# Mixing stage of a six-layer transformer forward pass: B projections, compression and value tiles ahead of the attention units, gate and branch tiles woven in between

## The reference

```
n = rms_norm(h, norm_g)
aq, ak, av, bq, bkc, bvc, bks, bvs, bkw, bvw, bgate, cq, ck, cv, ga, gb, gc = split(n @ w_in)
ya = diff_attention(aq, ak, av)                 # 4 heads, two softmaxes each
yb = nsa_attention(bq, compress(bkc), compress(bvc), bks, bvs, bkw, bvw, sigmoid(bgate))   # 8 heads, 3 kinds
yc = swa_sink_attention(cq, ck, cv)             # 8 heads
merged = sigmoid(ga)*(ya @ wb[0]) + sigmoid(gb)*(yb @ wb[1]) + sigmoid(gc)*(yc @ wb[2])
h = h + merged @ w_out
```

## Time and profile before

| what | value |
|---|---|
| median of three runs | 3616.49 us (3616.34 to 3617.01) |
| profiled execution, its own time | 3612.1 us |
| its span | 3610.3 us |
| mean granted TensorE clock | 0.959 of 2.4 GHz |
| TensorE busy | 3432.8 us, 95% |
| VectorE busy | 1848.2 us, 51% |
| ScalarE busy | 1561.2 us, 43% |
| GpSimd busy | 161.0 us, 4% |

### The profile page before, as it was taken

The page is one execution under the profiler, slowest core; times in us unless marked ns, Lnnn a source line. Parts: engine busy times, 40 slices in busy tenths (PEclk is TensorE's granted clock), DMA queues, the critical chain, the costliest instruction groups (busy, mean ns, idle before and its releaser), DMA issues.

```text
span 3610.3 us, 42172 instructions
## 1 busy us (share of the span) xinstructions
PE 3432.8 (95%) x17691; PEld 2906.6 (81%) x17691; DVE 1848.2 (51%) x2378; ACT 1561.2 (43%) x1908; POOL 161.0 (4%) x253
## 2 busy tenths in 40 slices
PE   8999999859999999999999999999999999999998
PEld 6898888647888888787988788878887788878886
DVE  4455454564454564544554545524545545434545
ACT  4344444334444444443344343356444443454444
POOL 0000000020000000000000000033000000131000
PEclk9999999879999999999999999869999999789999
DMA  6545555414555445554555455503554555413553
GB/s 205 189 165 178 187 186 189 144 35 150 189 180 189 161 162 189 177 187 163 170 174 188 151 188 169 165 24 98 174 187 164 178 193 158 130 47 117 186 189 112
DMA packets 329835, 576.39 MB, mean 160 GB/s; under 512 B 45034, under 2 KB 148561, under 8 KB 329517
## 3 DMA queue, kind: packets, MB, share of 16 engines
q1 hardware_dynamic: 327116, 566.71, 47.2%
q0 software_dynamic: 2384, 6.63, 0.6%
q10 hardware_dynamic: 144, 0.35, 0.0%
HBM read 571.53 MB, written 1.08 MB: 159 GB/s over the span
## 4 chain that ended last, share of the span: by engine, by line
PE 90%; DVE 6%; ACT 3%; issue 1%; DMA 0%; POOL 0%; DVEq 0%; SPq 0%; ACTq 0%; POOLq 0%
PE up L1584 19%; PE up L1586 19%; PE up L1585 19%; PE acc L1584 7%; PE acc L1586 7%; PE acc L1585 7%; DVE w_lo L891 2%; ACT w_hi L513 2%; PE acc L1742 1%; PE up L1847 1%; PE up L2055 1%; PE acc L1749 1%; PE acc L1743 1%; PE acc L1653 0%; PE acc L1669 0%
## 5 line engine op out<-in xcount | busy, mean ns | idle before, releaser
L891 DVE TENSOR_TENSOR w_lo<-raw,w_hi 128x2048 fp32r<-128x2048 f32 x543 | 1244.2, 2292 | 1334.9 <-ACT w_hi L513 1329.8
L513 ACT ACTIVATE w_hi<-raw 128x2048 fp32r<-128x2048 f32 x543 | 1040.0, 1917 | 1507.5 <-PE up L1586 1127.8
L1584 PE MATMUL up<-w_hi,xT_hi 128*128 128x512 f32 (+2 forms) x2404 | 935.1, 389 | 49.8 <-DVE xT_lo L1003 28.0
L1586 PE MATMUL up<-w_hi,xT_lo 128*128 128x512 f32 (+2 forms) x2404 | 930.8, 387 | 0.0
L1585 PE MATMUL up<-w_lo,xT_hi 128*128 128x512 f32 (+2 forms) x2404 | 930.3, 387 | 0.0
L1584 PEld LDWEIGHTS up<-w_hi,xT_hi 128*128 128x128 f32 x2404 | 459.9, 191 | 143.7 <-issue 37.6
L1586 PEld LDWEIGHTS up<-w_hi,xT_lo 128*128 128x128 f32 x2404 | 460.0, 191 | 90.4
L1585 PEld LDWEIGHTS up<-w_lo,xT_hi 128*128 128x128 f32 x2404 | 460.4, 192 | 88.5
L1584 PE MATMUL acc<-w_hi,ff_hi 128*128 128x512 f32 (+1 forms) x1280 | 497.8, 389 | 3.5 <-DVE ff_lo L1022 3.5
L1586 PE MATMUL acc<-w_hi,ff_lo 128*128 128x512 f32 (+1 forms) x1280 | 491.8, 384 | 0.0
L1585 PE MATMUL acc<-w_lo,ff_hi 128*128 128x512 f32 (+1 forms) x1280 | 491.2, 384 | 0.0
(11 more groups left out here) (276 smaller groups left out, 2500.2 us busy)
## 6 DMA issues: line engine op xcount, KB each, us to landing
raw<-in_ffn_down SPq DMA_DIRECT2D x88, 1024.0 KB, 4.8
raw<-in_ffn_gate SPq DMA_DIRECT2D x80, 1024.0 KB, 5.0
raw<-in_ffn_up SPq DMA_DIRECT2D x80, 1024.0 KB, 5.0
raw<-in_ffn_wi SPq DMA_DIRECT2D x80, 1024.0 KB, 5.0
raw<-in_ffn_wo SPq DMA_DIRECT2D x44, 1024.0 KB, 4.8
raw<-in_w_in SPq DMA_DIRECT2D x44, 1024.0 KB, 5.1
raw<-in_conv_w_in SPq DMA_DIRECT2D x24, 1024.0 KB, 5.0
raw<-in_w_branch SPq DMA_DIRECT2D x12, 1024.0 KB, 4.9
```

The source lines that it names most:

```text
L513: nc.scalar.activation(w_hi[n % RING][:], raw[n % RING][:], ACT.Copy).then_inc(hi_ready, 1)
L891: nc.vector.tensor_tensor(w_lo[n % RING][:], raw[n % RING][:], w_hi[n % RING][:].bitcast(F32), ALU.subtract).then_inc(lo_ready, 1)
L1584: pe.matmul(ps, lh, rh, start=start, stop=False)
L1586: return pe.matmul(ps, ll, rh, start=False, stop=stop)
```

## The change

The norm ahead of the mixing stage joins `XS`. The stage opens with A's values (`first_pair` into `up2`, `up3`); a matmul of ones with the scaled diagonal gives `rstd` along the free axis (`rb`), by which DVE scales feature-major results as it takes them out. The projection tiles are regrouped: the B keys of both kinds in one tile (`kk`), all values with the 24 gate columns in two tiles of 408 columns (`v`), C's keys as one of 128 columns (`ck`). A table `GROUPS` gives each group its kind, its banks (now only `up0` and `up1`, but for A's values) and how many evictions ACT and DVE signal for it; before a group's first matmul PE waits (`evicted`) until the earlier holders of its banks are out. The hidden layer's four tiles stand in a row in `up0` and `up1`. Gates are token-major and kept in six SBUF buffers, so that they no longer wait for the branch product; a gate group has four pieces of 12 matmuls of 512 columns, a branch group two.

`AHEAD` (q0, q1, kk, hid0, hid1, v) runs before unit 0; the second compression product, C's queries and keys and the gate and branch groups are pieces of the unit loop from step 7 on, one per step to step 45, and five behind it. On ACT and DVE a piece that ends a tile runs `consumed`, and behind it, in a group's last piece, the eviction. The merged result is token-major, is transposed by PE (16 transposes) and split from PSUM, and the end of the stage does `turn_x(0)` for the next norm. GpSimd's copies for the compression input wait for the KC tile's eviction as before.

```diff
-XS = ("ffn", "mla", "ple")
+XS = ("ffn", "mla", "mix", "ple")
...
+                t = [cols_tile(w[rows, :], 4, W_AV, 512) for rows in half]
+                t += [up_tile(w, W_BC)] + [up_tile(w, W_AQ + CW * j) for j in range(4)]
                 t += [query_tile(w, W_BQ, j) for j in range(2)]
...
+                t += [(KD, CW, [(slice(P * j, P * j + P), kpn(w)[:, :, at:at + P]) for j, at in enumerate((W_BS, W_BW))])]
+                t += [up_tile(w1[v, 1024 * h:1024 * h + 1024, :], 0) for v in range(2) for h in range(2)]
+                t += [(4, 408, [(slice(P * j, P * j + P), kpn(w[rows, :])[:, :, at + P:at + 2 * P])
+                                for j, at in enumerate((W_BS, W_BW, W_CKV))]
+                       + [(slice(384, 408), kpn(w[rows, :])[:, :, W_BG:W_BG + 24])]) for rows in half]
+                t += [query_tile(w, W_CQ, j) for j in range(2)] + [cols_tile(w, KD, W_CKV, P)]
...
+        GROUPS = [("av", "pair", (2, 3), 0, 1), ("bc", "ws", (0,), 0, 1)]
+        GROUPS += [(name, "ws", (b,), 0, 1) for name, b in (("aq0", 1), ("aq1", 0), ("ak0", 1), ("ak1", 0), ("q0", 1),
+                                                            ("q1", 0), ("kk", 1))]
+        GROUPS += [("hid0", "hid", (0,), 1, 0), ("hid1", "hid", (1,), 1, 0), ("v", "pair", (0, 1), 1, 1),
+                   ("hidT", "", (0,), 0, 1), ("cmp", "", (1,), 0, 1), ("q2", "ws", (0,), 0, 1), ("q3", "ws", (1,), 0, 1),
+                   ("ck", "k", (0,), 0, 1), ("g0", "pair", (0, 1), 1, 0), ("ya", "", (0, 1), 0, 2),
+                   ("g1", "pair", (0, 1), 1, 0), ("g2", "pair", (0, 1), 1, 0), ("b0", "b", (0, 1), 0, 1),
+                   ("b1", "b", (0, 1), 0, 1)]
+        GROUPS += [(f"g{j}", "pair", (0, 1), 1, 0) for j in (3, 4, 5)]
+        GROUPS += [(f"b{j}", "b", (0, 1), 0, 1) for j in (2, 3, 4, 5)]
...
+            BEFORE[name] = [holder[b] for b in in_banks if b in holder]
+            holder.update((b, name) for b in in_banks)
...
+        AHEAD = parts_in("q0", "q1", "kk", "hid0", "hid1", "v")
+        for j, piece in enumerate(parts_in("hidT", "cmp", "q2", "q3", "ck", "g0", "ya", "g1", "g2", "b0", "b1", "g3", "g4",
+                                           "g5", "b2", "b3", "b4", "b5")):
+            PIECES.setdefault(min(7 + j, STEPS), []).append(piece)
...
+                act.wait_ge(rs_ready, seen.next(rs_ready))
+                for i in range(TILE_AT["q0"]):
                     consumed(n0 + i)
+
+                def dense(name, part):
+
+                    done = tile_end(name, part)
+                    if done is not None:
+                        consumed(n0 + done)
+                    if part + 1 < KINDS[KIND[name]]:
+                        return
+                    if name in ("hid0", "hid1"):
+                        v = int(name[3])
+                        nc.scalar.activation(hid[:, v, :], up[BANKS[name][0]][0:2 * NCMP, 0:CW],
+                                             ACT.Gelu_apprx_tanh).then_inc(dense_act, 1)
+                    elif name == "v":
+                        for t in range(NT):
+                            last = nc.scalar.activation(gB[:, t, :], up[t][:, 384:408], ACT.Sigmoid,
+                                                        scale=rstd[:, t:t + 1])
+                        last.then_inc(dense_act, 1)
...
+                    elif name[0] == "g":
+                        for t in range(NT):
+                            last = nc.scalar.activation(gates_of[int(name[1])][:, t, :], up[t][:], ACT.Sigmoid,
+                                                        scale=rstd[:, t:t + 1])
+                        last.then_inc(dense_act, 1)
...
+                def scaled(dst, name, m=2):
+
...
+                    nc.vector.tensor_tensor(dst, src, r, ALU.mult).then_inc(dense_dve, 1)
...
+                def blocks(v):
+
+                    if v == 0:
+                        dve.wait_ge(kc2_in, seen.next(kc2_in, 16 * 8))
...
+                def dense(name, part):
+
+                    done = tile_end(name, part)
+                    if done is not None:
+                        consumed(n0 + done)
+                    if part + 1 < KINDS[KIND[name]]:
                         return
...
+                    if name in places:
+                        scaled(places[name], name)
...
+                    elif name == "v":
+                        dve.wait_ge(dense_act, ACT_IN * s[1] + EVICTED["v"][0])
+                        for t in range(NT):
+                            last = nc.vector.tensor_scalar(BCV[:, t, 0:384], up[t][:, 0:384], rstd[:, t:t + 1], None, ALU.mult)
+                        last.then_inc(dense_dve, 1)
...
+                def merge(j):
+
+                    br, c = divmod(j, 2)
+                    dve.wait_ge(dense_act, ACT_IN * s[1] + EVICTED[f"g{j}"][0])
+                    cols = slice(FW * c, FW * c + FW)
+                    for t in range(NT):
+                        dst = merged[:, t, cols] if br == 0 else gates_of[j][:, t, :]
+                        last = nc.vector.tensor_tensor(dst, gates_of[j][:, t, :], up[t][:], ALU.mult)
+                    last.then_inc(dense_dve, 1)
+                    if br == 0:
                         return
...
+                    dve.wait_ge(dense_dve, DVE_IN * s[1] + EVICTED[f"b{j}"][1])
+                    for t in range(NT):
+                        last = nc.vector.tensor_tensor(merged[:, t, cols], merged[:, t, cols], gates_of[j][:, t, :], ALU.add)
+                    if br == 1:
+                        step(last)
+                    else:
+                        last.then_inc(merged_ready, 1)
...
+                for v in range(2):
+                    blocks(v)
+                for piece in AHEAD:
+                    dense(*piece)
...
+                def evicted(name):
+
+                    a, d = EVICTED[name]
+                    if a:
+                        pe.wait_ge(dense_act, ACT_IN * s[1] + a)
+                    if d:
+                        pe.wait_ge(dense_dve, DVE_IN * s[1] + d)
+
+                def dense(name, part):
+
+                    kind, b = KIND[name], BANKS[name][0]
+                    n = n0 + TILE_AT[name]
+                    if part == 0:
+                        for held in BEFORE[name]:
+                            evicted(held)
+                    if part == 0 and kind or kind == "hid" or (kind == "pair" and part == 2):
+                        pe.wait_ge(lo_ready, seen.next(lo_ready))
...
+                    elif kind == "pair":
+                        h, t = divmod(part, 2)
+                        last = token_half(n + h, 4, 408 if name == "v" else FW, 4 * h, t,
+                                          [up[j][:, 0:408] if name == "v" else up[j][:] for j in range(2)], h == 0, h == 1)
...
+                    o = [up[2 + h % 2][:, P * t:P * t + P] for t in range(NT)]
...
+                first_pair(n0, FW, [up[2][:], up[3][:]])
+                pe.wait_ge(diag_ready, seen.next(diag_ready))
+                pe.matmul(acc[0][:, 0:TOK], ones[:], diag[:].rearrange("p t n -> p (t n)"), start=True,
+                          stop=True).then_inc(rb_done, 1)
+                for piece in parts_in("bc", "aq0", "aq1", "ak0", "ak1"):
+                    dense(*piece)
...
+                for piece in AHEAD:
+                    dense(*piece)
...
+                    for piece in PIECES.get(i, ()):
+                        dense(*piece)
                 pe.wait_ge(nmax_ready, seen.next(nmax_ready, 2))
+                for piece in PIECES[STEPS]:
+                    dense(*piece)
+                pe.wait_ge(olo_ready, seen.next(olo_ready, 2))
                 for c in range(2):
...
+                    pe.wait_ge(merged_ready, seen.next(merged_ready))
+                    for k in range(4):
+                        for t in range(NT):
+                            at = (k % 2) * TOK + t * P
+                            last = pe.transpose(up[2 * (1 - c) + k // 2][:, at:at + P],
+                                                merged[:, t, FW * c + P * k:FW * c + P * k + P], ident)
+                        if k % 2:
+                            last.then_inc(merged_turned, 1)
+                downs = [(n0 + MIX_DOWN + j, ff_hi[:, j // 2, 2 * (j % 2):2 * (j % 2) + 2, :],
+                          ff_lo[:, j // 2, 2 * (j % 2):2 * (j % 2) + 2, :]) for j in range(4)]
+                for j in range(2):
                     pe.wait_ge(lo_ready, seen.next(lo_ready))
                     pe.wait_ge(mlo_ready, seen.next(mlo_ready))
...
+                    down_matmuls(*downs[j], j == 0, False)
+                pe.wait_ge(lo_ready, seen.next(lo_ready))
+                pe.wait_ge(mlo_ready, seen.next(mlo_ready))
+                down_half(*downs[2], 0, False)
+                pe.wait_ge(lo_ready, seen.next(lo_ready))
+                pe.wait_ge(mlo_ready, seen.next(mlo_ready))
+                down_half(*downs[3], 0, True)
```

(45 more changed lines are left out.)

500 lines of the change are left out of this document (201 added, 299 removed).

## The result

The changed kernel takes 3702.77 us (median of four, 3698.93 to 3704.01); the kernel before, run beside it, 3616.41 us (3611.27 to 3617.01). The ratio is 1.024, with a 95% interval of 1.0222 to 1.0258: slower, as forecast, but by 86 us where 44.5 were forecast, and 2.8 us above the range. The profiled execution has a span of 3700.2 us at a mean granted clock of 0.950.

What follows compares the result with a forecast made beforehand. TensorE was taken as the bound, 90% of the chain. Stages of 381.4 us gave, with the next FFN's gain, +9.3 us; clock falls +35; on the profiled 3612.1, plus 4.4 to the median, 3661 us, range 3625 to 3700.

Steps and rivals of the forecast that it cites:

- The fill: Between the value tiles and the first unit's transposes: splits, values' eviction, scores, softmax and normalisation take 9.4 us against 5.3.
- The waits in the loop and up to b3: TensorE's added waits for bank evictions at gate, C key and branch groups: 32.6 us a stage, bounds 25 to 40.
- the two bare ones behind it: Two waits at branch groups behind the attention loop, with no unit's work beside them: 11.8 us a stage.
- The waits at the boundaries: Groups share up0 and up1, so TensorE waits for evictions standing behind tile splits; 2.5 to 5.9 us each in and behind the loop.
- Rival S: Waits at bank boundaries lie beside the unit's work, so 41 us of waits and 15 of clock go twice: 3548 us, chance 0.12.
- the six of 2.5 to 2.7: Six short waits per stage in the attention loop, at gate groups and C's keys, counted with no fall of TensorE's clock.
- rival C: TensorE's clock falls at the short waits too: six more falls twice, +30 us, 3691 us, chance 0.20.
- The gate and branch pieces: Pieces woven into the attention loop: 36 x 2.88 = 103.7 us fall to 36 x 2.72 = 98 us.
- The seven falls: Seven waits a stage of 3.8 us or longer, at b0 to b5 and g5, each lose 2.5 us of clock: 17.5 us.
- The next FFN: Behind the mixing stage the FFN starts without a gap and at the full clock, counted as a gain of 2.5 us twice.
- The table's load: ScalarE's sigmoid table loads behind the split in 1.28 us without a drain; with the skill page's drain the total would be 3678.
- Rival D: The clock stays high through the loop's first ten steps: 14 us less twice, 3633 us, chance 0.06.

Runs made afterwards that it cites:

- the first experiment: Changed kernel with the eviction of a finished group ahead of the next weight tile's split on ScalarE and VectorE: 3560.6 us, 0.9854 of the kernel before.
- The filled kernels: Changed kernel with added identity matmuls in TensorE's boundary waits: 3643.4 us with 10 to 27 at all waits, 3690.6 with 10 or 11 at five short ones.
- The woven value tiles: Four value pieces moved into loop steps 0, 1, 3 and 5: 3540.8 us with evictions ahead of splits, 3683.0 us in the changed kernel's order.

## Why the forecast was right in sign and short in size

Right, by its own steps, in the second stage: ak1 ends after 42.5 us (42.3 forecast). kk starts 16.7 later (17.0), after a wait of 5.2 (5.5). v takes 11.7 with its fall (11.3), its matmuls at 0.187 us (0.183). The fill takes 8.9 us (9.4), steps 4 to 9 with the first pieces 29.5 (29.6). The waits in the loop and up to b3 sum to 34.0 us (32.6), the two bare ones behind it to 11.3 (11.8), and the merged transposes wait 6.0 (7.1 in the forecast's terms: split, products and sums). The waits at the boundaries were the term that decides, and the first experiment shows it: without them the same dense work is 1.5% faster than before. Rival S described that kernel at 3548, not this one.

The step that failed is the clock's: "the six of 2.5 to 2.7 lie at the 2.6 that was harmless, so I leave them out". The spells behind those six waits are 34.1 us at half in the first stage and 27.3 in the second, and TensorE is busy for 29.2 and 25.2 us of them: half of that is 27 us in both stages where the forecast had nothing, close to the 30 of rival C. The measured excess of the profiled execution (3702.0 with its surroundings against 3656.4) is 46, so this is about six tenths of it. The filled kernels bear out the rule by which it is counted.

What misled me was the pause in the earlier trace rows: 2.6 us of idle time with the clock kept. It was one instance. The same pause, from the same code with the same large matmuls ahead, comes again in the other layer of the kernel before, from 3579.96 to 3582.59, and there the clock fell. The first microsecond in which TensorE works again, after the one and after the other:

```profile
2795.00:2796.00 1.00, 0.60 (x3) 1.00 0.67 221
...
3582.00:3583.00 1.00, 0.41 (x1) 0.51 0.00 0
```

The trace of before has more of both kinds: a fall behind 1.98 us of idle time (2502.97) and behind 2.31 (2588.92 and 3375.97), none behind 2.98 (2013.01), and none behind the first stage's instance of the very wait of 3.10 (2528.66) that lost it at 3313 in the earlier trace rows. So waits of 2 to 3 us lose the clock sometimes, with or without a unit's small matmuls ahead, and equal ones fare differently: 2.51 us lost it at 3231.85 and kept it at 3284.86. What decides stays open; a price for the fall at each, and not nothing, could have been read from the rows of before.

The rest is smaller. The gate and branch pieces were priced from the middle of a stream, 0.227 us a matmul. Over all 432 of them in a stage it is 0.239 from start to start, the step from each piece to the next unit included and time at the half clock taken at half: a piece is 2.87 us and not 2.72, 5 us a stage. The seven falls that were counted at 2.5 us, 17.5 a stage, cost 17.0 and 14.7 by the busy time in their spells, and those at kk and v 5.1 and 4.5 where 5 was counted, so these terms were of the right size. v starts 1.8 us late: the three issues ahead of its load's last part had been passed over in the wait's price. g0's wait is 1.1 us longer. The next FFN does not start at once, but after 1.9 us for its `xT_lo`, and with a spell of 3.4 at half; the forecast had neither, and took a gain of 2.5 twice for their absence. And 4.2 us of the difference lie ahead of the first mixing stage, where runs of the same code differ by as much (kk of the first stage starts at 2270.6 to 2276.3 in six kernels that are equal up to there).

The table's load was rightly priced by the row: it starts 0.02 us behind the split and takes 1.28. The Trainium skill's drain of 1.38 us (ScalarE: Activation LUTs, What ACT_TABLE_LOAD costs) is not in this trace, between the load's end at 3230.47 and the sigmoid at 3230.48 least of all.

Rival D put the bare steps at 14 us a stage. The woven value tiles give back 10, with the fill wait: the mechanism holds, the price was high.

## What to carry to other kernels

Where groups share their PSUM banks one after the other, write the eviction ahead of whatever the evicting engine owes to later tiles; here that order alone moved the time by 142 us. When you price an idle spell of TensorE, count the clock at waits of 2 us too: half of the busy time in the spell behind it. And look for every instance of a wait before you call it harmless; here the one on which the forecast rested had lost the clock in the other layer. Work taken out of a loop that overlaps it leaves bare steps behind, and these are paid for in waits and in clock.

## What the runs showed of the hardware that was not expected

The clock fell at waits of 2.5 to 3.8 us, in eleven of twelve cases, and stayed for 3.4 to 10.2 us at half behind each; it kept or lost its level behind equal waits of 2.51 us, and in the kernel before behind equal ones of 2.63 us. The part of such a spell that lies in idle time cost nothing. An fp32 matmul of the identity on 128 columns took 0.23 us at the full clock, in two records. A load of 1 MB that was cut into four DMAs of 256 KB began its last part 3.4 us after its buffer was free, since the first three issues on SP's queue took 0.37, 1.94 and 0.93 us.
